# Hybrid decoder step on one core: the weight sum of the feed-forward block by an accumulating DMA, its three differences on VectorE, queues reordered

## The chip, the cores and the metric

The kernel is written for one core of a Trainium2 chip and runs on one core. The metric is the device time of one execution in microseconds, median of several runs; lower is better.

## The reference, cut to what matters

One inference step of a two-layer decoder, for 512 prompt tokens and 8 single-token samples with the same weights. Layer 0 mixes by attention and mLSTM heads, layer 1 by a recurrent block; after each mixer comes a SwiGLU feed-forward block, and after each of these four sub-layers a layer normalization. The change touches the first product of the feed-forward block alone:

```python
def ffn(u, li):
    gate, up = jnp.split(u @ w_ffn_in[li], 2, axis=-1)     # 1024 x 5632
    return (jax.nn.silu(gate) * up) @ w_ffn_out[li]        # 2816 x 1024

xp = post_norm(xp, ffn(up, li), mod_p[5], li, 1)
```

All of it is float32. The kernel keeps that precision by splitting each operand into a high part (rounded to fp32r) and a low part (the rest) and adding three matmuls: high x high, high x low, low x high.

## The kernel before

Activations lie transposed, features on the 128 partitions; the 520 columns (512 tokens, 8 samples) are two column halves of HT = 260. TensorE multiplies a 128x128 weight tile by 260 columns at a time.

**Stages.** The work goes in stages; each stage is a list of weight chunks. The feed-forward block of layer l has four: fi{l}0 (11 chunks), fo{l}0 (8), fi{l}1 (11), fo{l}1 (8). A chunk of fi holds the weights of 128 gate and 128 up features, for all 1024 input features: 1 MB in one of four raw buffers (NRAW), loaded by SyncE in two DMAs as [partition, k of 8, gate or up, 128]. Chunk c of the whole program uses raw buffer c mod 4, and its load waits (raw_free) until the chunk four before is through with its low parts.

**Seven products instead of eight.** In fi, all chunks but 0 and 1 of fi{l}0 (40 in all, `split_seven`) are computed by a Strassen-like scheme (the Winograd form). The chunk is a 2x2 block matrix: a11 (k 0 to 3, gate), a12 (k 4 to 7, gate), a21 (k 0 to 3, up), a22 (k 4 to 7, up), each 128x512 numbers in SBUF. The token matrix is likewise cut in 2x2, by feature halves and column halves. Seven block products, each of 4 k times 3 = 12 matmuls, replace eight. Their weight sides, in the order b = 0 to 6, are a11; S = a21 + a22; S - a11; a12 - (S - a11); a11 - a21; a12; a22.

**Who makes what.** For each block b, ScalarE makes the high part (`hi7(c, b)`, L1335) from its source in the raw buffer or in wsum, and VectorE the low part (`lo7(c, b)`, L2257). Before the change S is made on GpSimd into a buffer of its own, wsum (`weight_sum` part 0, L961), and a11 - a21 too, in the place of a21 (part 1, L963). VectorE makes the other two right behind `lo7(c, 0)` and `lo7(c, 1)`: S - a11 in the place of a11 (L2263), a12 minus that in the place of wsum (L2265). The buffer wsum lies in the memory of the second weight slot (whi[1]), so part 0 waits until its last user there is through: for the first chunk of fi{l}1 that is the last chunk of fo{l}0, for the first one of fi10 chunk 1. High and low parts have one buffer for each block, which holds the chunk being multiplied; `block_free` makes `hi7(n, b)` wait for product b of the chunk before.

**Evacuation.** Products accumulate in PSUM. Of a chunk c, ScalarE copies three intermediate sums out of the way (`copy_product` 0, 1, 2, L1522), after products 0, 1 and 2; TensorE starts blocks 2, 3 and 4 only after them. VectorE adds product sums in `add12` (L2562, after product 3) and `add22` (L2570, after product 4); block 6 waits for add22. Then ScalarE applies silu to both column halves (`silu_sums`, L1531 and L1534), VectorE multiplies by the up half (`gated_first` L2577, `gated_second` L2585), ScalarE makes the high part of the result (`high_h`, L1486) and VectorE its low part (`low_h`, L2538). For chunks 0 and 1 of fi{l}0 the corresponding steps are silu_of and gated_h.

**The order is written out by hand.** Every engine works through its queue in order. In the steady loop (step c, next chunk n = c + 1) ScalarE's queue is: copy 0, hi 6 of c, hi 0 of n, copy 1, hi 1 of n, copy 2, high_h of c - 1, hi 2 to 5 of n, keep (fi{l}0 only, L1415), both silus. VectorE's: gated_second of c - 1, lo 5 and 6 of c, lo 0 and 1 of n with a difference behind each, add12, low_h of c - 1, add22, lo 2 and 3 of n, gated_first, lo 4 of n.

GpSimd's queue, `ffn_sums(r)`, runs once per layer: small work on the samples, both parts for chunk 2, the four token sums (`token_sum`, 128x1040, L979 to L988), and then, for t = 0 to 7, both parts for chunk 3 + t and `keep_normalized(t)` (L1018, 128x520: part of what the residual needs later), and the parts for the eleven chunks of fi{l}1. Before and after that it works in the layer normalizations (L916 to L948).

**Starts.** Chunks 0 and 1 of fi{l}0 are multiplied while VectorE is still making the low tokens (`gained` L2479 and `low_tokens` L2486), tile by tile; TensorE follows them (`first_two_by_halves`, L3157). At the end of fo{l}0 the parts of the first chunk of fi{l}1 are made in the loop over its last two chunks: blocks 0 to 3 while chunk 7 is multiplied, 4 to 6 behind it.

## Time and profile before

| | us |
|---|---|
| median of 3 runs | 1551.78 |
| lowest, highest | 1549.71, 1552.03 |
| the profiled execution | 1551.36 |
| its span, first to last instruction | 1549.3 |

| engine | busy us | share of the span | instructions |
|---|---|---|---|
| TensorE (PE) | 1376.3 | 89% | 11764 |
| VectorE (DVE) | 1070.4 | 69% | 1599 |
| ScalarE (ACT) | 700.7 | 45% | 1180 |
| GpSimd (POOL) | 456.3 | 29% | 397 |

The chain that ended last is 34% VectorE, 28% TensorE, 5% ScalarE, 1% GpSimd. The mean granted TensorE clock is 0.95 of full. "L2257" is line 2257 of the kernel; "[0.36 <-ACT silb L1531]" behind an instruction means that its engine sat idle for 0.36 us before it, and what ended that. Matmuls overlap: one is shown as 0.28 us long and the next starts 0.12 us after it.

### The profile page before, as it was taken

Reading aid. Unit: us, or ns where it says so; the run is one execution under the profiler, and the core shown is the slowest. Engines: PE = TensorE matmul, PEld = TensorE weight load, DVE = VectorE, ACT = ScalarE, POOL = GpSimd, SP = SyncE. Lnnn points to the kernel's source line nnn. Section 1 sums busy time; section 2 is a strip of 40 time slices with the busy share of each in tenths; the row PEclk is TensorE's granted clock in tenths of the full one; section 3 lists DMA queues with packets and bytes.
Section 4 is the critical chain, followed back from the end, with each engine's and each line's share of the span. In section 5 each row is a group of like instructions: output and inputs, shape, how many; then the busy total and the mean of one; then the engine's idle time right before and its main releaser. Section 6 shows DMA issues by size and latency. Waiting matters only on the chain.

```text
span 1549.3 us, 30521 instructions
## 1 busy us (share of the span) xinstructions
PE 1376.3 (89%) x11764; PEld 1308.6 (84%) x11764; DVE 1070.4 (69%) x1599; ACT 700.7 (45%) x1180; POOL 456.3 (29%) x397
## 2 busy tenths in 40 slices
PE   4999978889997798989999989988968899899996
PEld 4899957666887698989999889988867889899995
DVE  4523268754757998449984888895769983499756
ACT  1211153234423666226653366892436661266524
POOL 2000031311174332012214536553553320133154
PEclk8999999899897899999999999998988999999998
DMA  9632296668330122323323212313402324233311
GB/s 319 213 95 55 84 334 236 234 244 303 112 109 1 55 81 75 105 80 109 100 76 111 82 41 90 108 36 98 136 1 55 100 71 115 82 85 97 94 38 56
DMA packets 213509, 175.04 MB, mean 113 GB/s; under 512 B 9079, under 2 KB 183932, under 8 KB 213252
## 3 DMA queue, kind: packets, MB, share of 16 engines
q1 hardware_dynamic: 208448, 160.13, 33.5%
q0 software_dynamic: 4800, 13.23, 2.5%
q8 instruction: 72, 1.18, 0.3%
q14 instruction: 49, 0.40, 0.1%
q10 hardware_dynamic: 140, 0.09, 0.0%
HBM read 167.87 MB, written 5.63 MB: 112 GB/s over the span
## 4 chain that ended last, share of the span: by engine, by line
DVE 34%; PE 28%; ACT 5%; issue 2%; POOL 1%; ACTq 0%; DVEq 0%; POOLq 0%
PE ps L3148 15%; DVE wlo L2257 12%; PE ps L3307 5%; PE ps L3157 4%; PE ps L3177 3%; DVE gn L2479 2%; ACT whi L1335 2%; DVE wsum L2265 2%; DVE raw L2263 2%; DVE hb L2577 2%; DVE wlo L2249 1%; DVE HL L2538 1%; DVE xc L2706 1%; DVE tL L2553 1%; DVE UL L2486 1%
## 5 line engine op out<-in xcount | busy, mean ns | idle before, releaser
L3307 PE MATMUL ps<-UH,whi 128*128 128x260 f32 x640 | 186.9, 292 | 28.6 <-DVE hb L2570 28.5
L1322 ACT ACTIVATE whi<-raw 128x1408 fp32r<-128x1408 f32 (+3 forms) x64 | 101.3, 1582 | 241.4 <-PE ps L3148 186.8
L2257 DVE TENSOR_TENSOR wlo<-raw,whi 128x512 fp32r<-128x512 f32 x200 | 187.1, 936 | 8.9 <-ACT whi L1335 2.2
L961 POOL TENSOR_TENSOR wsum<-raw 128x512 f32<-128x512 f32 x40 | 54.5, 1361 | 438.7 <-DVE wlo L2257 262.0
L3307 PE MATMUL ps<-UL,whi 128*128 128x260 f32 x640 | 183.4, 287 | 0.0
L3307 PE MATMUL ps<-UH,wlo 128*128 128x260 f32 x640 | 182.7, 285 | 0.0
L3307 PE MATMUL ps<-tH,whi 128*128 128x260 f32 x480 | 139.9, 292 | 34.8 <-DVE tL L2546 13.5
L1335 ACT ACTIVATE whi<-raw 128x512 fp32r<-128x512 f32 x200 | 126.4, 632 | 65.9 <-DVE raw L2263 37.3
L2249 DVE TENSOR_TENSOR wlo<-raw,whi 128x1408 fp32r<-128x1408 f32 (+3 forms) x64 | 130.6, 2040 | 36.4 <-ACT whi L1322 35.6
L3307 PEld LDWEIGHTS ps<-UH,whi 128*128 128x128 f32 x640 | 123.5, 193 | 35.5 <-issue 34.3
L3307 PE MATMUL ps<-tH,wlo 128*128 128x260 f32 x480 | 139.2, 290 | 0.0
L3307 PE MATMUL ps<-tL,whi 128*128 128x260 f32 x480 | 138.8, 289 | 0.0
L3148 PE MATMUL ps<-UH,whi 128*128 128x260 f32 x624 | 126.8, 285 | 6.9 <-DVE wlo L2249 6.9
L3148 PE MATMUL ps<-UH,wlo 128*128 128x260 f32 x624 | 126.1, 284 | 0.0
L3148 PE MATMUL ps<-UL,whi 128*128 128x260 f32 x624 | 126.0, 284 | 0.0
L3307 PEld LDWEIGHTS ps<-tH,whi 128*128 128x128 f32 x480 | 93.3, 194 | 37.2 <-issue 29.2
L3307 PEld LDWEIGHTS ps<-UL,whi 128*128 128x128 f32 x640 | 123.4, 193 | 0.0
L3307 PEld LDWEIGHTS ps<-UH,wlo 128*128 128x128 f32 x640 | 123.3, 193 | 0.0
L3148 PEld LDWEIGHTS ps<-UH,whi 128*128 128x128 f32 x624 | 96.8, 190 | 8.1 <-DVE wlo L2249 8.1
L3148 PE MATMUL ps<-HH,whi 128*128 128x260 f32 x484 | 97.4, 283 | 0.0
L3148 PE MATMUL ps<-HH,wlo 128*128 128x260 f32 x484 | 97.1, 282 | 0.0
L3148 PE MATMUL ps<-HL,whi 128*128 128x260 f32 x484 | 97.1, 282 | 0.0
(552 smaller groups left out, 3723.0 us busy)
## 6 DMA issues: line engine op xcount, KB each, us to landing
raw<-in_w_ada SPq DMA_DIRECT2D x96, 512.0 KB, 6.7
raw<-in_w_ffn_in SPq DMA_DIRECT2D x88, 512.0 KB, 5.1
raw<-in_w_in_even SPq DMA_DIRECT2D x24, 512.0 KB, 4.8
raw<-in_w_ffn_out SPq DMA_DIRECT2D x32, 384.0 KB, 4.1
raw<-in_w_ffn_out SPq DMA_DIRECT2D x32, 320.0 KB, 3.2
raw<-in_w_in_odd SPq DMA_DIRECT2D x20, 512.0 KB, 4.5
raw<-in_w_out_odd SPq DMA_DIRECT2D x16, 320.0 KB, 3.6
page<-in_cache_k POOLq DMA_DIRECT2D x16, 256.0 KB, 5.1
```

The lines of the kernel that those rows point to most:

```text
L961: ins = pool.tensor_tensor(wsum[:], a21, a22, ALU.add)
L1322: ins = nc.scalar.activation(whi[w][:, 0:f], raw[c % NRAW][:, 0:f], ACT.Identity)
L1335: nc.scalar.activation(seven_block(b)[0], seven_source(c, b), ACT.Identity).then_inc(seven_hi, 1)
L2249: ins = v.tensor_tensor(wl_[:, 0:f], raw[c % NRAW][:, 0:f], wh[:, 0:f].bitcast(F32), ALU.subtract)
L2257: v.tensor_tensor(low, seven_source(c, b), high.bitcast(F32), ALU.subtract).then_inc(seven_lo, 1)
L2263: ins = v.tensor_tensor(a11, wsum[:], a11, ALU.subtract)
L2265: ins = v.tensor_tensor(wsum[:], a12, a11, ALU.subtract)
L2479: v.scalar_tensor_tensor(gn_of(r, hf)[:, t, 0:HALF], xT[:, t, hf, 0:HALF], gain, rstd[:, hf, 0:HALF], ALU.mult, ALU.mult).then_inc(n_ready, 1)
L3148: ins = T.matmul(ps(g)[:, hf, 0:HT], wt(k, m), x[:, k, hf], start=(k == 0 and wt is wh and x is xh), stop=(k == s.k - 1 and wt is wl_))
L3157: ins = T.matmul(ps(g)[:, hf, 0:HT], wt(k, m), xt[:, k, hf], start=(k == 0 and wt is wh and xt is xh), stop=(k == s.k - 1 and wt is wl_), ...
L3177: ins = T.matmul(ps(g)[:, hf, 0:HT], w(k, m), x[:, k, hf], start=(i == 0 and w is wh and x is xh), stop=(i == s.k - 1 and w is wl_))
L3307: ins = T.matmul(out, wt[:, k], x, start=(b in (0, 1) and k == 0 and wt is wh and x is xh), stop=(k == 3 and wt is wl_), skip_group_check= ...
```

## The change

GpSimd no longer computes on the weights. It issues, for each of the 40 chunks, one DMA that reads a22 again from DRAM and adds it to a21 in the raw buffer, so that S stands in the place of a21; ScalarE waits for that DMA before hi 1. wsum is gone, and with it the wait for its memory. The sums of chunks 2 and 3 are issued ahead of the token sums, the others one chunk earlier than before relative to keep_normalized. VectorE makes all three differences in place: S - a11 over a21, a12 minus that over a11, a22 minus S - a11 (which is a11 - a21) over a21. ScalarE's and VectorE's queues are in another order: high_h and low_h come at the head of a step, keep before hi 2, the first silu between hi 3 and hi 4, the second between hi 4 and hi 5, lo 2 before add22. The whole diff:

```diff
--- before.py
+++ after.py
@@ -428,7 +428,6 @@
         tL = [at("tL0", [P, 4, HT], O_L, F32R), at("tL1", [P, 4, HT], O_L + 4 * HTB, F32R)]
         tL2 = [at("tL20", [P, 2, HT], O_L + 6 * HTB, F32R),
                nc.alloc_sbuf_tensor_at("tL21", [P, 2, HT], F32R, offset=CN0 + C_MASK * 4 + 2 * HTB)]
-        wsum = nc.alloc_sbuf_tensor_at("wsum", [P, 4, P], F32, offset=split_at + 4 * (SLOT + 1536))
         db = sml[:, 28:32]
 
         xr = at("xr", [P, KR, 2 * HT], 0)
@@ -456,7 +455,8 @@
 
         raw_loaded = [sem(f"raw_loaded{i}") for i in range(NRAW)]
         hi_done, lo_done = sem("hi_done"), sem("lo_done")
-        seven_hi, seven_lo, wsum_ready = sem("seven_hi"), sem("seven_lo"), sem("weight_sums_ready")
+        seven_hi, seven_lo = sem("seven_hi"), sem("seven_lo")
+        wsum_ready = [sem(f"weight_sum_ready{i}") for i in range(NRAW)]
         product_filled, copied, u3_used, pre_ready = sem("product_filled"), sem("product_copied"), sem("u3_used"), sem("pre_ready")
         wdiff_ready = sem("weight_differences_ready")
         silu_ready = sem("silu_of_sums")
@@ -543,7 +543,7 @@
 
             r = raw[c % NRAW][:].rearrange("p (k g m) -> p k g m", k=8, g=2)
             a11, a12, a21, a22 = r[:, 0:4, 0], r[:, 4:8, 0], r[:, 0:4, 1], r[:, 4:8, 1]
-            return (a11, wsum[:], a11, wsum[:], a21, a12, a22)[b]
+            return (a11, a21, a21, a11, a21, a12, a22)[b]
 
         def seven_block(b):
 
@@ -948,21 +948,13 @@
                     pool.tensor_tensor(x, x, mu[:, hf, 0:HALF], ALU.subtract).then_inc(d_ready, 1)
                     settled(pool, d_ready)
 
-            def weight_sum(n, part):
+            def weight_sum(n):
 
                 i = seven_index[n]
-                a11, a12, a21, a22 = (seven_source(n, b) for b in (0, 5, 4, 6))
-                if part == 0:
-                    pool.wait_ge(raw_loaded[n % NRAW], 32 * (n // NRAW + 1))
-                    if holder[n][1] not in seven_index:
-                        slot_free(pool, n, 1)
-                    if i >= 1:
-                        pool.wait_ge(seven_lo, 7 * i - 3)
-                    ins = pool.tensor_tensor(wsum[:], a21, a22, ALU.add)
-                else:
-                    ins = pool.tensor_tensor(a21, a11, a21, ALU.subtract)
-                ins.then_inc(wsum_ready, 1)
-                settled(pool, wsum_ready)
+                s = chunk_stage[n]
+                pool.wait_ge(raw_loaded[n % NRAW], 32 * (n // NRAW + 1))
+                pool.dma_start(seven_source(n, 1), weight_view(s)[s.chunks.index(n)][:, 4:8, 1],
+                               accum_op=ALU.add).then_inc(wsum_ready[n % NRAW], 16)
 
             def gn_samples(r, hf):
 
@@ -997,8 +989,8 @@
                 gn_samples(r, 0)
                 gn_samples(r, 1)
                 link(pool.tensor_tensor(db, B9[:, r + 1, 4:8, 0], B9[:, r + 1, 0:4, 0], ALU.subtract))
-                weight_sum(n0[2], 0)
-                weight_sum(n0[2], 1)
+                weight_sum(n0[2])
+                weight_sum(n0[3])
                 token_sum(r, 0)
                 token_sum(r, 1)
                 token_sum(r, 2)
@@ -1007,12 +999,11 @@
                 pool.wait_ge(rstd_ready, 2 * r + 2)
                 pool.wait_ge(ulo_ready, 8 + 16 * (r + 1))
                 for t in range(KD):
-                    for part in range(2):
-                        weight_sum(n0[3 + t], part)
+                    if t < KD - 1:
+                        weight_sum(n0[4 + t])
                     keep_normalized(t)
                 for n in n1:
-                    for part in range(2):
-                        weight_sum(n, part)
+                    weight_sum(n)
 
             def keep_normalized(t):
                 pool.tensor_tensor(xT[:, t], xT[:, t], rstd[:], ALU.mult).then_inc(kept_n, 1)
@@ -1328,10 +1319,10 @@
                 i = seven_index[c]
                 act.wait_ge(raw_loaded[c % NRAW], 32 * (c // NRAW + 1))
                 block_free(act, c, b)
-                if b in (1, 4):
-                    act.wait_ge(wsum_ready, 2 * i + (1 if b == 1 else 2))
-                if b in (2, 3):
-                    act.wait_ge(wdiff_ready, 2 * i + b - 1)
+                if b == 1:
+                    act.wait_ge(wsum_ready[c % NRAW], 16 * len([x for x in seven_index if x <= c and x % NRAW == c % NRAW]))
+                if 2 <= b <= 4:
+                    act.wait_ge(wdiff_ready, 3 * i + b - 1)
                 nc.scalar.activation(seven_block(b)[0], seven_source(c, b), ACT.Identity).then_inc(seven_hi, 1)
                 settled(act, seven_hi)
 
@@ -1522,14 +1513,18 @@
                 nc.scalar.activation(dst, ps(g)[:, src, 0:HT], ACT.Identity).then_inc(copied, 1)
                 settled(act, copied)
 
-            def silu_sums(s, c):
+            def silu_first(s, c):
 
                 i = seven_index[s.chunks[c]]
-                g = s.g0 + 2 * c
                 sil = ff_buffers(s, c)[0]
                 act.wait_ge(pre_ready, i + 1)
                 nc.scalar.activation(sil[:, 1], sil[:, 1], ACT.Silu).then_inc(silu_ready, 1)
                 settled(act, silu_ready)
+
+            def silu_second(s, c):
+
+                g = s.g0 + 2 * c
+                sil = ff_buffers(s, c)[0]
                 wait_filled(act, g)
                 free(nc.scalar.activation(sil[:, 0], ps(g)[:, 0, 0:HT], ACT.Silu), g)
                 act.wait_ge(freed[g % NGRP], g // NGRP + 1)
@@ -1566,30 +1561,35 @@
                         for b in range(5):
                             hi7(ch[3], b)
                         hi7(ch[3], 5)
-                        silu_sums(s, 2)
+                        silu_first(s, 2)
+                        silu_second(s, 2)
                         first = 3
                     for c in range(first, s.n):
                         k = k0 + c
                         n = ch[c + 1] if c + 1 < s.n else None
-                        copy_product(s, c, k, 0)
                         if c > 0:
                             hi7(ch[c], 6)
+                            high_h(s, c - 1, k - 1)
+                        copy_product(s, c, k, 0)
                         if n is not None:
                             hi7(n, 0)
                         copy_product(s, c, k, 1)
                         if n is not None:
                             hi7(n, 1)
                         copy_product(s, c, k, 2)
-                        if c > 0:
-                            high_h(s, c - 1, k - 1)
+                        if hf == 0:
+                            keep(2 * l, c - 3)
                         if n is not None:
-                            for b in range(2, 6):
-                                hi7(n, b)
+                            hi7(n, 2)
+                            hi7(n, 3)
                         else:
                             hi(f0)
-                        if hf == 0:
-                            keep(2 * l, c - 3)
-                        silu_sums(s, c)
+                        silu_first(s, c)
+                        if n is not None:
+                            hi7(n, 4)
+                        silu_second(s, c)
+                        if n is not None:
+                            hi7(n, 5)
                     high_h(s, s.n - 1, k0 + s.n - 1)
                     hi(f0 + 1)
                     s = st[f"fo{l}{hf}"]
@@ -2256,15 +2256,17 @@
                 dve.wait_ge(seven_hi, 7 * seven_index[c] + b + 1)
                 v.tensor_tensor(low, seven_source(c, b), high.bitcast(F32), ALU.subtract).then_inc(seven_lo, 1)
                 settled(dve, seven_lo)
-                if b < 2:
-                    a11, a12 = seven_source(c, 0), seven_source(c, 5)
-                    dve.wait_ge(wsum_ready, 2 * seven_index[c] + 2)
-                    if b == 0:
-                        ins = v.tensor_tensor(a11, wsum[:], a11, ALU.subtract)
-                    else:
-                        ins = v.tensor_tensor(wsum[:], a12, a11, ALU.subtract)
-                    ins.then_inc(wdiff_ready, 1)
-                    settled(dve, wdiff_ready)
+            def difference(c, j):
+
+                a11, a12, a21, a22 = (seven_source(c, b) for b in (0, 5, 4, 6))
+                if j == 0:
+                    ins = v.tensor_tensor(a21, a21, a11, ALU.subtract)
+                elif j == 1:
+                    ins = v.tensor_tensor(a11, a12, a21, ALU.subtract)
+                else:
+                    ins = v.tensor_tensor(a21, a22, a21, ALU.subtract)
+                ins.then_inc(wdiff_ready, 1)
+                settled(dve, wdiff_ready)
 
             g = use["tb"]
             wait_filled(dve, g)
@@ -2599,11 +2601,14 @@
                         if l == 1:
                             lo7(ch[2], 0)
                         lo7(ch[2], 1)
+                        difference(ch[2], 0)
+                        difference(ch[2], 1)
                         token_low(l, 0)
                         low_h(s, 0, k0)
                         gated_h(s, 1, k0 + 1)
                         token_low(l, 1)
                         lo7(ch[2], 2)
+                        difference(ch[2], 2)
                         low_h(s, 1, k0 + 1)
                         lo7(ch[2], 3)
                         token_low(l, 2)
@@ -2615,7 +2620,10 @@
                         add22(s, 2)
                         lo7(ch[3], 0)
                         lo7(ch[3], 1)
+                        difference(ch[3], 0)
+                        difference(ch[3], 1)
                         lo7(ch[3], 2)
+                        difference(ch[3], 2)
                         lo7(ch[3], 3)
                         gated_first(s, 2)
                         lo7(ch[3], 4)
@@ -2627,19 +2635,21 @@
                             gated_second(s, c - 1)
                             lo7(ch[c], 5)
                             lo7(ch[c], 6)
+                            low_h(s, c - 1, k - 1)
                         if n is not None:
                             lo7(n, 0)
                             lo7(n, 1)
+                            difference(n, 0)
+                            difference(n, 1)
                         add12(s, c)
-                        if c > 0:
-                            low_h(s, c - 1, k - 1)
+                        if n is not None:
+                            lo7(n, 2)
                         add22(s, c)
                         if n is not None:
-                            lo7(n, 2)
+                            difference(n, 2)
+                            lo7(n, 3)
                         else:
                             lo(f0)
-                        if n is not None:
-                            lo7(n, 3)
                         gated_first(s, c)
                         if n is not None:
                             lo7(n, 4)
@@ -2656,6 +2666,11 @@
                         else:
                             for b in range(4 * (c - s.n + 2), 7 if c == s.n - 1 else 4):
                                 lo7(s.c0 + s.n, b)
+                                if b == 1:
+                                    difference(s.c0 + s.n, 0)
+                                    difference(s.c0 + s.n, 1)
+                                if b == 2:
+                                    difference(s.c0 + s.n, 2)
                 ln_round(2 * l + 1)
 
             def per_tile(col, n=NS):

```

## Rows read from the trace of the kernel before

**Rows 1.** Chain that ended last: start us, length us, engine, tile, line, instructions.

```profile
538.80 11.87 PE ps L3307 x84
...
622.03 7.89 PE ps L3177 x66
...
629.93 55.27 PE ps L3148 x462
...
808.43 7.89 PE ps L3177 x66
```

**Rows 2.** Waits: who waited for whom; us in total, times, longest.

```profile
PE ps L3307 <- DVE hb L2570: 28.5, 32, 2.3
```

**Rows 3.** VectorE in time, fi01: start, length, line, out<-in, [idle before].

```profile
734.84 1.67 DVE L2257 TENSOR_TENSOR wlo<-raw,whi 128x512 fp32r<-128x512 f32 x1
...
737.00 2.65 DVE L2257 TENSOR_TENSOR wlo<-raw,whi 128x512 fp32r<-128x512 f32 x3
...
739.69 0.69 DVE L2263 TENSOR_TENSOR raw<-wsum,raw 128x512 f32<-128x512 f32 x1
...
745.44 1.66 DVE L2257 TENSOR_TENSOR wlo<-raw,whi 128x512 fp32r<-128x512 f32 x1
```

**Rows 4.** GpSimd in time, the same stretch.

```profile
734.51 1.44 POOL L961 TENSOR_TENSOR wsum<-raw 128x512 f32<-128x512 f32 x1 [7.47 <-DVE wlo L2257]
...
736.03 1.62 POOL L963 TENSOR_TENSOR raw<-raw 128x512 f32<-128x512 f32 x1
```

**Rows 5.** VectorE in time, fi00.

```profile
529.34 0.64 DVE L2577 TENSOR_TENSOR hb<-hb,silb 128x260 f32<-128x260 f32 x1 [1.09 <-ACT silb L1531]
...
588.11 1.38 DVE L2577 TENSOR_TENSOR hb<-hb,silb 128x260 f32<-128x260 f32 x1 [0.37 <-ACT silb L1531]
```

**Rows 6.** GpSimd in time, fi00.

```profile
578.79 1.65 POOL L1018 TENSOR_TENSOR xT<-xT,rstd 128x520 f32<-128x520 f32 x1
```

**Rows 7.** TensorE in time, starts of fi00 and fi10.

```profile
505.79 0.28 PE L3307 MATMUL ps<-UH,whi 128*128 128x260 f32 x1
...
530.19 0.39 PE L3307 MATMUL ps<-tH,whi 128*128 128x260 f32 x1 [1.74 <-ACT ps L1522]
...
1147.40 0.28 PE L3307 MATMUL ps<-UH,whi 128*128 128x260 f32 x1
...
1162.51 0.56 PE L3307 MATMUL ps<-tH,whi 128*128 128x260 f32 x1 [13.50 <-DVE tL L2546]
...
1183.69 0.38 PE L3307 MATMUL ps<-tH,whi 128*128 128x260 f32 x1 [1.00 <-ACT ps L1522]
```

**Rows 8.** GpSimd in time, starts of fi01 and fi10.

```profile
685.41 1.29 POOL L961 TENSOR_TENSOR wsum<-raw 128x512 f32<-128x512 f32 x1 [81.12 <-PE ps L3148]
...
1147.80 1.29 POOL L961 TENSOR_TENSOR wsum<-raw 128x512 f32<-128x512 f32 x1 [14.30 <-PE ps L3157]
```

**Rows 9.** TensorE in time, start of fi01.

```profile
689.62 0.41 PE L3307 MATMUL ps<-tH,whi 128*128 128x260 f32 x1 [3.01 <-DVE wlo L2257]
```

**Rows 10.** Windows: us, busy (x) of PE, PEld, DVE, ACT, POOL; PEclk; DMA.

```profile
689.00:693.00 4.00, 2.79 (x12) 2.49 (x12) 3.71 (x7) 3.08 (x5) 0.99 (x1) 0.61 0.00 0
```

**Rows 11.** DMA issues: out<-in, queue, count, KB each, median us to landing.

```profile
raw<-in_w_ffn_in SPq DMA_DIRECT2D x88, 512.0 KB, 5.1
...
page<-in_cache_k POOLq DMA_DIRECT2D x16, 256.0 KB, 5.1
...
Cs<-in_state_C POOLq DMA_DIRECT2D x1, 1024.0 KB, 12.8
```

**Rows 12.** Groups by form, ScalarE: count, busy us, mean ns.

```profile
L1486 ACT ACTIVATE HH<-hb 128x520 fp32r<-128x520 f32 x44 | 28.2, 641 | 12.9 <-DVE hb L2585 6.3 <-DVE hb L2532 5.3
```

**Rows 13.** VectorE in time, layer normalization before fi00.

```profile
491.39 2.49 DVE L2479 SCALAR_TENSOR_TENSOR gn<-xT,G,rstd 128x256 f32<-128x256 f32 x1
```

**Rows 14.** GpSimd in time, a DMA issue in the middle stage.

```profile
203.03 0.54 POOL L836 DMA_DIRECT2D out_k_prompt<-ktok  x1 [2.23 <-ACT vtok L1088]
```

**Rows 15.** VectorE in time, beside that issue.

```profile
203.21 0.68 DVE L1820 TENSOR_TENSOR rowc<-rows,rowc 4x512 f32<-4x512 f32 x1
```

## The prediction

> **What bounds the kernel now.** I read the chain of work that ended last first, for the order of the stages and their lengths, then the waits of TensorE, then each engine's instructions in order of time in single chunks. Each layer has a feed-forward block in two halves, fi{l}0 and fi{l}1, of 11 chunks each. Chunks 0 and 1 of fi{l}0 are computed directly; the other nine and all eleven of fi{l}1 go through seven block products, 84 matmuls a chunk, 40 chunks in all. Dense matmuls go at 55.27 us / 462 = 0.1196 us [rows 1], so 84 take 10.05 us: TensorE's floor for a chunk, a block of 12 being 1.44 us.
>
> In fi{l}1 a chunk takes 745.44 - 734.84 = 10.60 us [rows 3], and in that stretch VectorE's instructions follow each other with no idle time: VectorE sets the pace and TensorE waits a little each time for the addition of L2570 before its block 6, in both halves together 28.5 us in 32 waits [rows 2]. VectorE doesn't really have that much to do. A low part of 128x512 takes 0.69 us where GpSimd is still, as the difference at 739.69 [rows 3], but 1.66 to 1.67 us beside GpSimd's first addition, and the first of the three at 737.00, beside its second, takes 2.65 - 2 x 0.72 = 1.21 us [rows 3, 4] (0.72 is 0.69 with the step to the next). These two cost 0.98 + 0.52 = 1.50 us a chunk. Without them VectorE would need 9.10 us.
>
> In fi{l}0 the eight last chunks take longer: from block 6 of chunk 3 (538.80) to the end (622.03) it is 83.2 us for seven chunks' worth of work, 11.9 a chunk [rows 1]. GpSimd does a third instruction per chunk, keep_normalized [rows 6], and VectorE both loses time to it and sits idle for silu_first on ScalarE [rows 5], which is queued behind four high parts and keep.
>
> Two more places. At the start of fi{l}1 the sum block cannot be written before TensorE is through with the last chunk of fo{l}0, since wsum lies in the second slot: GpSimd waits 81 us for it and adds at 685.41 [rows 8]; TensorE stands 3.01 us [rows 9] and comes back at the lower level of its clock, 0.61 granted [rows 10], matmuls every 0.21 us. At the start of fi10 the same wait ends at 1147.80 [rows 8], all four token sums are queued behind it, and TensorE stands 13.50 us [rows 7].
>
> **The change part by part.**
>
> 1. *Two GpSimd additions per chunk go; the third difference comes to VectorE.* In fi{l}1 VectorE's chunk becomes 10.60 - 1.50 + 0.72 = 9.82 us, under TensorE's 10.05. What is late next is TensorE itself, if the new order holds. I walked one chunk with block 0 at 0 and products done at 1.6, 3.1, 4.5, 5.9, 7.4, 8.8 and 10.2: gated_second at 0.2, lo 5, lo 6 and low_h to 2.8, lo 0 to 3.6, lo 1 pinned by its high part (product 1) at 4.2 to 4.9, two differences to 6.3, add12 to 6.8, lo 2 to 7.5, add22 to 8.0, against block 6 at 8.6. Then difference 2, lo 3, gated_first and lo 4 to 10.6, 0.4 behind, which the pinned lo 1 takes up again. No wait on TensorE is left, with 0.6 us to spare. ScalarE has 8 us of work at most and no long idle wait in it. So fi{l}1 goes from 808.43 - (629.93 + 55.27) = 123.2 us [rows 1] to 11 x 10.05 + 0.6 for uneven spots = 111.1 us. That includes the stall at its start: the sum now needs no slot, blocks 0 to 3 are made during the last chunk of fo{l}0, and by the same walk block 4's low part is there 3 us before its turn. Gain 12.1 us, twice: 24.2.
>
> 2. *fi{l}0, chunks 3 to 10.* keep_normalized stays on GpSimd and now runs some 9 us after chunk start, when the load behind it has landed (5.1 us, [rows 11]), beside VectorE's low parts and differences. Its price lies between 0.52 and 0.98 us, as for the two instructions of [rows 3, 4]; the upper is the nearer since a two-SBUF-input instruction is then under way nearly always. I take 0.95. silu_first comes before two of the high parts, so the wait of [rows 5] goes. From block 6 of chunk 3 to that of chunk 9 there are six chunks of 9.82 and five keeps: 58.9 + 4.8 = 63.7 us, still VectorE's, then block 6 and the last chunk on TensorE, 11.1. Together 74.8 against 83.2: gain 8.4, twice: 16.8. The copy of ScalarE's keep hides as before.
>
> 3. *The new order at the entry to that loop.* For chunk 3, copy_product 0 used to be the next thing after silu_second; TensorE waited 1.74 us for it (block 2 at 530.19, [rows 7]). Now high_h(2) stands ahead of it, and that waits for gated_first (529.34, 0.64 long, [rows 5]), lo 4 (0.69) and gated_second (at most 0.64) on VectorE and takes 0.64 itself [rows 12]: 2.3 to 2.6 us later, and 0.7 more for difference 2 on VectorE's queue, and up to 0.98 if a keep falls there. TensorE would stand 1.7 + 2.7 to 1.7 + 4.2 us, say 4.8. After 3.01 us at the handover the clock came back low [rows 9, 10], after 1.74 here it had not; so I expect the low level for about as long as there, some 30 matmuls at 0.21 instead of 0.12, 2.8 us. As part of the delay is taken up before block 6 (before it TensorE waited 2 us there as well), I put 3.7 us at block 6 of chunk 3, bounds 0 and 6. Loss 3.7, twice: 7.4.
>
> 4. *Start of fi{l}0.* Layer 0: the two additions go from the time in which VectorE makes the low tokens that TensorE follows one by one: about 2 x 0.9 = 1.8 us gained; two differences now on VectorE's busy stretch cost 1.4, the two additions gone later give back 1.1: net +1.5. Layer 1: the walk from block 0 of chunk 2 to block 2 of chunk 3 took 1183.69 - 1147.40 = 36.3 us and in layer 0, where the slot was free, 530.19 - 505.79 = 24.4 [rows 7]. The difference, 11.9, goes; but token sum 0 is now no longer held back and falls onto the low tokens, as in layer 0, where one 0.48 us instruction took 2.49 [rows 13]: -2.0, and -0.3 for the differences. Net +9.6. Layers together +11.1.
>
> 5. *The accumulating DMA.* Nothing in the trace adds in a DMA. Landing: the nearest in size is a page of 256 KB, 5.1 us; the far end is 1 MB in 4096 short rows, 12.8 us [rows 11]. I take 7. It has time: the raw buffer of chunk n is freed at lo 6 of chunk n - 4, its load lands about 6 us later, and hi 1 of chunk n comes three chunks and 1.4 us after that freeing: 3 x 10.05 + 1.4 - 6.5 = 25 us for the sum. At the start of fi10 GpSimd is free to issue it at 1147.80 - 14.30 = 1133.5 [rows 8], and ScalarE wants it some 3 us before block 0 of chunk 2 begins at 1147.40 [rows 7], 10.6 us later; TensorE's need is another 5 us away. Cost nothing, as long as it lands in those times. Issue: GpSimd spends 0.54 us on one [rows 14]. Whether that takes VectorE's time as an addition does: the 0.68 us instruction with two SBUF inputs at 203.21 ran beside such an issue at its usual length [rows 14, 15]. It is on 4 partitions only, but I take 0; the upper bound is 0.98 per issue.
>
> Sum: 24.2 + 16.8 - 7.4 + 11.1 = 44.7 us. The profiled execution took 1551.36 us (span 1549.3), the median of the runs is 1551.78, 0.4 more. 1551.8 - 44.7 = 1507.1 us.
>
> **The rivals.**
>
> A. *The issue on GpSimd takes VectorE's time like an addition.* For it: every GpSimd computation does [rows 3, 4]; against it: [rows 14, 15], weak evidence. At 0.75 a chunk VectorE is at 10.57 in fi{l}1, hardly better than 10.60, which costs 0.52 x 11 x 2 = 11.4 us, and 0.75 x 6 x 2 = 9 in fi{l}0: 1527.5 us (1535 at 0.98).
>
> B. *No low clock and little delay at chunk 3* (part 3 costs nothing): 1499.7 us.
>
> C. *Slower: the DMA sum lands late.* Per chunk T = (6.5 + L - 1.4) / 3 once L passes 25 us; the gain of 44.7 is eaten over 36 chunks at 1.25 us more a chunk, that is L of about 29 us; at L = 33, T is 12.7, and 36 x 2.65 = 95 us come on top, with some 20 each at the starts: 1640 us. For it: the adding must read both sides and no row has its price; against: twice the worst landing of [rows 11] is 25.6. The Trainium skill's page "DMA: Bandwidth & Descriptors" (Anatomy of one DMA) would give 2.6 us for a plain transfer of this size issued on GpSimd; the row has 5.1.
>
> D. *VectorE still sets the pace by the order of its queue* (the walk has only 0.23 us per chunk and 0.6 at block 6): 10.3 instead of 10.05 in fi{l}1 costs 5.5: 1513 us.
>
> E. *keep_normalized costs VectorE its whole length*, 1.65 us [rows 6] where I take 0.95. Against it: a 1.44 us addition cost 0.98, the next 0.52 [rows 3, 4]. It would cost 0.7 x 5 x 2 = 7 us: 1514. The Trainium skill's page "SBUF — State Buffer" (Who interferes with whom) has this rule: of a VectorE instruction with two inputs in SBUF and a GpSimd instruction that reads SBUF, the one that starts second waits for the first to end. In the rows above the loss always stays under the length of the GpSimd instruction.
>
> F. *Nothing gained*, for a cause that I don't see, within 0.2%: about 1552.
>
> **How the numbers follow.** Forecast with part 3 as told, 0.48; D 0.08; E 0.04; B 0.10; A 0.18; C 0.08; F 0.04. The likeliest is 1507. The range takes in B and most of A: 1498 to 1528, leaving out C, F and a little at each end, 0.2. A measurement of this kernel tells 0.2% from no change. Faster: 0.48 + 0.08 + 0.04 + 0.10 + 0.18 = 0.88; same 0.04; slower 0.08.
>
> **What would show it.** In fi{l}1: chunks of 10.05 us, no wait of TensorE for L2570, all low parts at 0.69, handover without the stall. Chunks of 10.5 with low parts over 0.9 beside a GpSimd issue: A. ScalarE waiting for the DMA before the high part of block 1 in every chunk: C. In fi{l}0: low parts slow once a chunk, chunks of 10.8 falling to 10.05 at the end; TensorE standing over 4 us before block 2 of chunk 3 and then 0.5 to 0.6 granted. At 1147: the 13.50 us gone to about 4. The forecast is wrong above all if the landing of the DMA is far over 13 us, or if the clock falls elsewhere.

## The result, and the profile after

The changed kernel takes 1525.28 us (median of 4 runs, 1523.42 to 1531.36) against 1550.94 before in the same comparison: a ratio of 0.984, 95% interval 0.981 to 0.987. That is 1.6% less, clear of the scatter, and inside the range given, but 18 us over the forecast of 1507: of the 44.7 us expected, 25.7 came. The profiled execution took 1526.53 us, its span is 1524.9 (before 1549.3), so the two spans differ by 24.4 us.

The second halves did what was forecast. From the chain of work that ended last, of the changed kernel (start us, length us, what), to be read against [rows 1]:

```profile
637.07 55.25 PE ps L3163 x462
692.33 110.79 PE ps L3322 x924
803.11 7.89 PE ps L3192 x66
...
1326.82 110.81 PE ps L3322 x924
```

All eleven chunks of fi01 are one unbroken run of 924 matmuls, 110.79 us, a chunk every 10.07. The handover from fo00 is without a wait. Nothing of VectorE's or ScalarE's is in it. GpSimd and VectorE in one of these chunks (start us, length us, engine, line, operation, tiles, count, idle time before; L956 is the accumulating DMA's issue):

```profile
740.93 1.29 POOL L956 DMA_DIRECT2D raw<-in_w_ffn_in  x1 [8.74 <-DMA raw<-in_w_ffn_in]
751.05 1.28 POOL L956 DMA_DIRECT2D raw<-in_w_ffn_in  x1 [8.82 <-DMA raw<-in_w_ffn_in]
...
750.67 0.69 DVE L2267 TENSOR_TENSOR raw<-raw 128x512 f32<-128x512 f32 x1
751.40 0.69 DVE L2257 TENSOR_TENSOR wlo<-raw,whi 128x512 fp32r<-128x512 f32 x1
752.12 0.43 DVE L2579 TENSOR_TENSOR hb<-hb,silb 128x260 f32<-128x260 f32 x1
```

The low part at 751.40 lies wholly inside the issue of 1.28 us and takes its usual 0.69. An issue by itself takes nothing from VectorE. It does take GpSimd 1.28 us, where the plain one of [rows 14] took 0.54. The landing, from the table of DMA issues (KB each, us to landing):

```profile
raw<-in_w_ffn_in SPq DMA_DIRECT2D x88, 512.0 KB, 5.1
raw<-in_w_ffn_in POOLq DMA_DIRECT2D x40, 256.0 KB, 4.6
```

4.6 us, 7.5 at most over the 40; the forecast took 7 and had 25 to spend. No engine waits for it.

The first halves did not do it. What TensorE waited for (engine, line, released by: us in total, times, longest):

```profile
PE ps L3322 <- ACT ps L1513: 22.9, 10, 5.5
PE ps L3322 <- DVE wlo L2257: 18.8, 2, 9.6
```

The wait for add22 [rows 2], 28.5 us before, has all but gone. In its place stand L1513, copy_product 0, before block 2 of chunk 3 and of later chunks of the first halves, and L2257 before block 2 of chunk 2, once per layer. Single waits and the clock behind the first two, in windows (stretch, length, busy us of each engine with the instructions, granted clock):

```profile
521.27 0.56 PE L3322 MATMUL ps<-tH,whi 128*128 128x260 f32 x1 [9.19 <-DVE wlo L2257]
539.86 0.58 PE L3322 MATMUL ps<-tH,whi 128*128 128x260 f32 x1 [5.39 <-ACT ps L1513]
565.11 0.38 PE L3322 MATMUL ps<-tH,whi 128*128 128x260 f32 x1 [1.63 <-ACT ps L1513]
590.00 0.58 PE L3322 MATMUL ps<-tH,whi 128*128 128x260 f32 x1 [2.41 <-ACT ps L1513]
...
1156.40 0.56 PE L3322 MATMUL ps<-tH,whi 128*128 128x260 f32 x1 [9.62 <-DVE wlo L2257]
```

```profile
521.00:525.00 4.00, 3.73 (x17) 3.76 (x18) 3.76 (x8) 1.31 (x3) 0.00 (x0) 0.50 0.31 39
...
539.00:543.00 4.00, 3.14 (x14) 3.15 (x15) 3.79 (x6) 2.44 (x6) 0.00 (x0) 0.50 0.41 121
```

And the cause, one chunk of fi00 on GpSimd and VectorE (L1009 is keep_normalized, L2579 gated_first):

```profile
559.72 1.30 POOL L956 DMA_DIRECT2D raw<-in_w_ffn_in  x1 [10.81 <-DMA raw<-in_w_ffn_in]
560.54 1.83 POOL L1009 TENSOR_TENSOR xT<-xT,rstd 128x520 f32<-128x520 f32 x1
...
559.45 0.69 DVE L2257 TENSOR_TENSOR wlo<-raw,whi 128x512 fp32r<-128x512 f32 x1
560.17 2.49 DVE L2579 TENSOR_TENSOR hb<-hb,silb 128x260 f32<-128x260 f32 x1
562.70 0.69 DVE L2257 TENSOR_TENSOR wlo<-raw,whi 128x512 fp32r<-128x512 f32 x1
```

keep is shown from 560.54, before the issue ends at 561.02, and gated_first, which takes 0.43 us elsewhere, takes 2.49. It lost 2.06 us, more than the 1.83 that keep is shown as long, and twice the 0.98 of an addition in [rows 3, 4]. gated_second, high_h and copy_product 0 follow from it in that order: hence the waits for L1513.

Fourteen of the sixteen keeps stand behind an issue like this one, and cost the VectorE instruction beside them 1.18 to 2.28 us, 1.85 on average. The last keep of each layer has no issue ahead of it and stands behind another keep; there the low part beside it takes 1.67 us, a loss of 0.98:

```profile
584.45 3.28 POOL L1009 TENSOR_TENSOR xT<-xT,rstd 128x520 f32<-128x520 f32 x2
...
586.61 1.67 DVE L2257 TENSOR_TENSOR wlo<-raw,whi 128x512 fp32r<-128x512 f32 x1
```

Where the 24.4 us of the two profiled executions lie, against the steps of the prediction (us, minus is faster; stretches between the same events in both traces):

| stretch | forecast | measured |
|---|---|---|
| up to gn of the second half, layer 0 (code unchanged) | 0 | +4.1 |
| gn to block 0 of chunk 2, layer 0 / layer 1 | -1.8 / +2.0 | -0.8 / +3.8 |
| block 0 of chunk 2 to block 6 of chunk 3 | +4.0 / -7.9 | +6.3 / -5.3 |
| block 6 of chunk 3 to the end of fi{l}0 | -8.4 / -8.4 | -2.3 / -3.0 |
| fi{l}1 | -12.1 / -12.1 | -12.5 / -12.5 |
| the rest | 0 | -2.2 |

The first row is no effect of the change, whose first instruction comes later. Here are the windows of 200 to 300 us, the kernel before first, then after:

```profile
200.00:300.00 100.00, 79.18 (x950) 62.49 (x951) 76.50 (x157) 36.80 (x92) 18.59 (x29) 0.90 0.77 264
```

```profile
200.00:300.00 100.00, 79.57 (x871) 63.12 (x871) 76.42 (x154) 35.77 (x89) 17.18 (x28) 0.85 0.77 266
```

950 matmuls at 0.90 granted against 871 at 0.85. One of the experiments below, keep_landed, had 0.85 there too and came to fi00 nearly as late. Over all fourteen traces the point at which the first row ends lies between 482.5 and 489.3 us. Where a few us matter, stages are compared below and not spans; the length of fi00 or fi10 is then from block 0 of chunk 2 to the end of the stage (116.1 us for fi00 before the change, 120.02 after).

### The profile page after: what moved, and what is told of

Its sections match the earlier page's. It is cut to its first block, busy times and chain, and to the rows that moved or that the text cites. A ratio compares the mean times of both kernels' runs of the same rounds, so it can differ in the third digit from the quotient of the medians.

```text
span 1524.9 us, 30410 instructions
## 1 busy us (share of the span) xinstructions
PE 1365.9 (90%) x11764; PEld 1303.8 (86%) x11764; DVE 1057.9 (69%) x1639; ACT 701.8 (46%) x1180; POOL 390.3 (26%) x357
## 3 DMA queue, kind: packets, MB, share of 16 engines
q8 instruction: 72, 1.18, 0.3%
## 4 chain that ended last, share of the span: by engine, by line
PE 44%; DVE 21%; ACT 4%; issue 1%; POOL 0%; ACTq 0%; DVEq 0%; POOLq 0%
PE ps L3322 21%; PE ps L3163 15%; PE ps L3172 4%; DVE wlo L2257 3%; PE ps L3192 3%; DVE gn L2481 2%; DVE UL L2488 1%; DVE wlo L2249 1%; DVE xc L2721 1%; DVE hb L2579 1%; DVE tL L2555 1%; DVE rstd L2454 1%; DVE xc L2756 1%; DVE raw L2267 1%; DVE xc L2755 1%
## 5 line engine op out<-in xcount | busy, mean ns | idle before, releaser
L1326 ACT ACTIVATE whi<-raw 128x512 fp32r<-128x512 f32 x280 | 177.6, 634 | 119.1 <-DVE raw L2267 58.1
L2257 DVE TENSOR_TENSOR wlo<-raw,whi 128x512 fp32r<-128x512 f32 x280 | 203.8, 728 | 15.8 <-ACT whi L1326 5.5
L3322 PE MATMUL ps<-UH,whi 128*128 128x260 f32 x640 | 182.7, 286 | 1.0 <-DVE hb L2572 1.0
L956 POOL DMA_DIRECT2D raw<-in_w_ffn_in x40 | 51.8, 1321 | 427.7 <-DMA raw<-in_w_ffn_in 425.4
L3163 PE MATMUL ps<-UH,whi 128*128 128x260 f32 x624 | 126.1, 283 | 6.9 <-DVE wlo L2249 6.9
L3322 PEld LDWEIGHTS ps<-tH,whi 128*128 128x128 f32 x480 | 93.5, 195 | 44.9 <-DVE wlo L2257 24.9
```

The costliest lines, as they stand in the source:

```text
L956: pool.dma_start(seven_source(n, 1), weight_view(s)[s.chunks.index(n)][:, 4:8, 1], accum_op=ALU.add).then_inc(wsum_ready[n % NRAW], 16)
L1326: nc.scalar.activation(seven_block(b)[0], seven_source(c, b), ACT.Identity).then_inc(seven_hi, 1)
L2257: v.tensor_tensor(low, seven_source(c, b), high.bitcast(F32), ALU.subtract).then_inc(seven_lo, 1)
L3163: ins = T.matmul(ps(g)[:, hf, 0:HT], wt(k, m), x[:, k, hf], start=(k == 0 and wt is wh and x is xh), stop=(k == s.k - 1 and wt is wl_))
L3322: ins = T.matmul(out, wt[:, k], x, start=(b in (0, 1) and k == 0 and wt is wh and x is xh), stop=(k == 3 and wt is wl_), skip_group_check= ...
```

## The experiments

Two theories stood against each other above all. Theory I in the expectations: keep_normalized, queued right behind an issue, is what costs VectorE 2 us and more. Theory III: the new order of the queues does it, high_h and low_h at the head of a step, with the wait that this makes at chunk 3. Each edit is against the changed kernel unless said otherwise; "before" was measured beside each group at 1551.75, 1552.74, 1550.45 and 1553.16 us, so medians of different groups that lie under 3 us apart are not told apart.

**keep_gap.** GpSimd holds each keep back until low part 6 of chunk 3 + t is made:

```diff
                         weight_sum(n0[4 + t])
+                    pool.wait_ge(seven_lo, 7 * seven_index[n0[3 + t]] + 7)
                     keep_normalized(t)
```

> The changed kernel with one wait more on GpSimd: keep_normalized(t) waits until low part 6 of chunk 3 + t is done, so it no longer runs directly behind the issue of an accumulating DMA, but 4 us or more after it. Theory I (in the changed kernel a keep costs VectorE 1.9 to 2.3 us because it is queued right behind the issue and takes the port before the issue is over): VectorE's loss per keep falls to between 0.5 and 1.0 us, TensorE's waits before block 2 in fi00 and fi10 (1.3 to 2.4 us a chunk) fall under 0.7, and the time falls by 8 to 12 us, to about 1515. Theory II (a keep costs whichever VectorE instruction comes behind it the rest of its own length, issue or no issue): a loss of 1.3 to 1.7 us per keep, and 1 to 4 us gained, 1522 to 1524.

1502.91 us (1500.06 to 1507.86), ratio 0.969 (0.965 to 0.973): one wait more, 22 us less, about twice the 8 to 12 expected, and 4 us under the forecast for the change. fi00 takes 109.51 us instead of 120.02, chunk 4 10.34, chunks 5 to 9 10.84 each. The same two engines in one chunk:

```profile
552.67 1.80 POOL L1010 TENSOR_TENSOR xT<-xT,rstd 128x520 f32<-128x520 f32 x1 [7.42 <-DVE wlo L2258]
554.77 1.30 POOL L956 DMA_DIRECT2D raw<-in_w_ffn_in  x1 [0.30 <-POOL xT L1010]
...
552.62 0.70 DVE L2541 TENSOR_TENSOR HL<-hb,HH 128x520 fp32r<-128x520 f32 x1
553.35 2.40 DVE L2258 TENSOR_TENSOR wlo<-raw,whi 128x512 fp32r<-128x512 f32 x2
```

Two low parts in 2.40 instead of 1.42 us: 0.98 lost, where the forecast had 0.95 and theory II 1.3 to 1.7. The issue right behind keep does no harm; it is keep right behind the issue that does.

**no_keep.** keep's multiplication is reduced to its first column, so that part of the computation is left out:

```diff
-                    keep_normalized(t)
+                    x = xT[:, t, :, 0:1]
+                    pool.tensor_tensor(x, x, rstd[:, :, 0:1], ALU.mult).then_inc(kept_n, 1)
```

> The changed kernel without the work of keep_normalized in fi00 and fi10: of each tile GpSimd multiplies only the first column of each half, so layer 0's and layer 1's residual is not normalized. What all contention by keep costs. From block 6 of chunk 3 to the end of fi00 80.8 us should become 6 x 10.05 + 11.6 = 72, in both layers 17 to 18 us, and 2 to 4 more where keeps 0 and 1 fall on chunk 2: 1503 to 1508. If the chunks of fi00 stay over 10.5 us, it is not keep that slows them but the new order.

1497.13 us (1496.79 to 1499.68), ratio 0.965, 6 us under the least expected. fi00 105.40, every chunk from chunk 4 on at 10.07. So the eight keeps of each layer cost the changed kernel 28 us together, and keep_gap 6.

**h_back.** high_h and low_h at their old places in the step, the rest as changed:

```diff
-                            high_h(s, c - 1, k - 1)
                         copy_product(s, c, k, 0)
 ...
                         copy_product(s, c, k, 2)
+                        if c > 0:
+                            high_h(s, c - 1, k - 1)
```

(and low_h behind add12 in the same way.)

> The changed kernel with high_h and low_h at their old places in the steady loop (behind copy 2 on ScalarE, behind add12 on VectorE), everything else as changed. Theory III (TensorE's stall before block 2 of chunk 3, 5.4 us, and those of 1.3 to 2.4 us in the chunks after it come from high_h, which stands ahead of copy 0 and waits for gated_second): the 5.4 us fall to 2 to 3 and the clock stays up, the smaller waits before block 2 vanish, 6 to 12 us gained: 1513 to 1519. Rival (VectorE sets the pace of fi00 and fi10 in any order): the waits only move to before block 6, and the time stays within 3 us of 1525. In fi01 and fi11, where nothing is late, no difference: 10.05 us a chunk.

1533.67 us (1529.13 to 1534.3): slower than the changed kernel, which neither side expected. The new place is worth 0.41 us in every chunk of the second halves: fi01's chunks take 10.48 instead of 10.07, and TensorE waits before block 6 for add22 again, a little at a time:

```profile
736.73 0.39 PE L3324 MATMUL ps<-UH,whi 128*128 128x260 f32 x1 [0.18 <-DVE hb L2573]
747.21 0.38 PE L3324 MATMUL ps<-UH,whi 128*128 128x260 f32 x1 [0.17 <-DVE hb L2573]
```

The wait before block 2 of chunk 3 is 3.27 us here and 5.39 in the changed kernel, but what was a wait there comes back at block 6 in each later chunk. In sum the old order makes fi00 2.1 us and fi10 0.9 us shorter than in the changed kernel: that much of the missing 19 us theory III can have, and no more. As the main cause of the lost time it has fallen.

**sum_on_gpsimd.** The sum by GpSimd in place, everything else as changed:

```diff
-                pool.dma_start(seven_source(n, 1), weight_view(s)[s.chunks.index(n)][:, 4:8, 1],
-                               accum_op=ALU.add).then_inc(wsum_ready[n % NRAW], 16)
+                a21, a22 = seven_source(n, 1), seven_source(n, 6)
+                pool.tensor_tensor(a21, a21, a22, ALU.add).then_inc(wsum_ready[n % NRAW], 16)
```

> The changed kernel with the sum made by GpSimd in place (128x512 in the raw buffer) instead of by the DMA: what the DMA alone is worth, beside the freed slot, the differences and the order. A chunk of fi01 becomes 9.82 us plus what the addition costs VectorE: 10.8 us at the 0.98 us that an addition cost before, 11.1 at its full length of 1.3. So fi01 and fi11 get longer by 8 to 12 us each, fi00 and fi10 by 0 to 5: 1543 to 1555. If the time stays near 1525, the DMA is worth nothing and the gain came from the slot and the order.

1537.47 us (1535.54 to 1538.92), 5.5 us better than the least expected. fi01 takes 116.49 us, a chunk 10.87:

```profile
742.51 1.29 POOL L957 TENSOR_TENSOR raw<-raw 128x512 f32<-128x512 f32 x1 [9.69 <-DMA raw<-in_w_ffn_in]
...
742.57 1.79 DVE L2258 TENSOR_TENSOR wlo<-raw,whi 128x512 fp32r<-128x512 f32 x1
```

The low part loses 1.10 us, and 9.82 + 1.10 = 10.92. The DMA is worth 5.7 us in each second half, and in the first halves nothing (119.08 with the addition, 120.02 with the DMA). The rows of fi00 say why: keep stands right behind the addition here and costs 0.99, gated_first taking 1.42 instead of 0.43:

```profile
558.75 1.64 POOL L1010 TENSOR_TENSOR xT<-xT,rstd 128x520 f32<-128x520 f32 x1
...
559.25 1.42 DVE L2580 TENSOR_TENSOR hb<-hb,silb 128x260 f32<-128x260 f32 x1
```

The addition ahead of it costs 0.98, together 1.97, and an issue with keep behind it in the same place cost 2.06. So behind a computation keep has its usual price, in an otherwise unchanged kernel, and what the DMA saves keep takes back.

**keep_landed.** This tells the issue from the place: keep waits until the DMA issued just before it has landed, and so falls neither right behind the issue nor beside low part 6:

```diff
                         weight_sum(n0[4 + t])
+                        pool.wait_ge(wsum_ready[n % NRAW], ...)   # the sum just issued
                     keep_normalized(t)
```

> The changed kernel, with one wait added on GpSimd: keep_normalized(t) waits until the accumulating DMA issued right before it has landed (4.6 us on average), so it no longer starts while that issue is under way, but also not beside low part 6 as in keep_gap. Theory I (what costs VectorE 2 to 3 us instead of 1 is that keep starts right behind the issue, wherever it falls): VectorE loses about 1.0 us per keep, chunks 4 to 9 of the first halves take 10.8 to 10.9 us, the stage fi00 109 to 111 us as in keep_gap (109.51), total about 1503 (1499 to 1508). Rival (keep_gap gained because keep falls beside low parts instead of beside gated_first and gated_second, from which high_h and copy 0 follow): the place of 4 to 6 us later decides, the stage stays at 115 us or more, total 1515 or more.

1508.4 us (1505.14 to 1515.03). fi00 111.85 and fi10 112.48 us. The profiled execution was the longest of the four and entered fi00 4.3 us later than keep_gap's, so the stages say it better: they are 8.2 and 7.3 us shorter than in the changed kernel.

```profile
543.87 1.30 POOL L956 DMA_DIRECT2D raw<-in_w_ffn_in  x1 [6.84 <-DMA raw<-in_w_ffn_in]
548.70 1.31 POOL L1011 TENSOR_TENSOR xT<-xT,rstd 128x520 f32<-128x520 f32 x1 [3.53 <-DMA raw<-in_w_ffn_in]
...
548.88 1.70 DVE L2542 TENSOR_TENSOR HL<-hb,HH 128x520 fp32r<-128x520 f32 x1
```

keep is 1.31 us long, low_h beside it loses 1.00. The distance from the issue decides, not what VectorE does at the time. The place has a small part too: the stages are 2.3 and 2.4 us longer than in keep_gap. All of that comes ahead of block 6 of chunk 3 (36.2 us from block 0 of chunk 2 in fi00, 33.4 in keep_gap), where three keeps fall here and one in keep_gap.

**keep_dve.** keep on VectorE, behind low part 4, on a semaphore of its own; GpSimd only issues:

```diff
                             lo7(n, 4)
+                            if hf == 0:
+                                keep_v(c - 2)
```

> The changed kernel with keep_normalized on VectorE, behind low part 4 of the next chunk, on a semaphore of its own; GpSimd only issues DMAs in these stages. Theory I: a two-input instruction of 128x520 costs VectorE 0.70 us where GpSimd is still, against 0.98 for the delay that the GpSimd keep costs in keep_gap. The chunk of chunks 4 to 9 becomes 9.82 + 0.70 = 10.5 us against 10.84 there, the stage fi00 about 107.5, total about 1499 (1496 to 1503). Rival (the delay by GpSimd's keep falls partly into VectorE's idle time, an own instruction does not): 10.8 us or more a chunk and 1503 or more.

1504.52 us (1502.59 to 1507.1): as keep_gap within the scatter, 5.5 above the 1499 expected. The loop came as worked out, nearly (10.63 a chunk for 10.5), so the rival's reason failed too; but chunk 3 takes 17.0 and 18.3 us in the two layers instead of 16.5: TensorE's wait before block 2 of chunk 3 is 5.39 us there, 4.64 in keep_gap.

**gap_copy_first.** keep_gap, and in chunk 3 alone copy_product 0 ahead of high_h:

```diff
+                            if hf == 0 and c == first:
+                                copy_product(s, c, k, 0)
                             high_h(s, c - 1, k - 1)
-                        copy_product(s, c, k, 0)
+                        if hf == 1 or c > first:
+                            copy_product(s, c, k, 0)
```

> keep_gap, and on ScalarE, in chunk 3 of the first halves alone, copy_product 0 stands ahead of high_h of chunk 2 again. Theory III, in the form that h_back leaves (the new place costs nothing inside the loop but one stall at its entry): the wait of 4.64 us before block 2 of chunk 3 falls to 1.5 to 2.5 us and TensorE stays at its full clock behind it, the first stage of each layer is 2.5 to 5 us shorter than in keep_gap (109.51 and 110.06), total 1494 to 1498. Rival (VectorE sets the pace of the loop from its first chunk on, so that the stall is only the place where TensorE waits for it): the wait goes elsewhere, the stages stay within 1 us, total 1501 to 1505.

1501.68 us (1500.28 to 1502.78), fi00 109.40 for 109.51, fi10 110.04 for 110.06: nothing, as the rival had it. The waits, the one of keep_gap first, then those here:

```profile
530.55 0.38 PE L3323 MATMUL ps<-tH,whi 128*128 128x260 f32 x1 [4.64 <-ACT ps L1514]
```

```profile
528.41 0.38 PE L3326 MATMUL ps<-tH,whi 128*128 128x260 f32 x1 [3.29 <-ACT ps L1514]
536.37 0.38 PE L3326 MATMUL ps<-UH,whi 128*128 128x260 f32 x1 [1.34 <-DVE hb L2576]
```

and the windows behind each, in the same order:

```profile
530.00:534.00 4.00, 3.45 (x17) 3.46 (x18) 3.83 (x6) 2.70 (x7) 2.76 (x2) 0.62 0.48 137
```

```profile
528.00:532.00 4.00, 3.24 (x25) 3.05 (x26) 3.83 (x6) 3.00 (x7) 1.81 (x1) 1.00 0.16 39
```

4.64 became 3.29 + 1.34, in sum the same. The clock granted behind it rose from 0.62 to 1.00, and that brought nothing either, since VectorE sets the pace from there on.

**gap_token_first.** keep_gap, and token sum 0 ahead of the two issues at the start instead of right behind them:

```diff
+                token_sum(r, 0)
                 weight_sum(n0[2])
                 weight_sum(n0[3])
-                token_sum(r, 0)
```

> keep_gap, and at the start of each first half GpSimd's token sum 0 stands ahead of the two DMA issues instead of right behind them. Theory I: token sum 0 then starts right behind no issue and costs VectorE about 2.0 us as in the kernel before, where the instruction beside it took 2.49 instead of 0.48 us, and not 3.5 (UL took 4.0). From the centering of the second half to block 0 of chunk 2, 1 to 2 us less per layer; total about 1500 (1498 to 1502). Rival (token sum 0 costs VectorE the same wherever it starts, or starts earlier and hits an instruction that TensorE follows more closely): no change or longer, 1502 to 1505.

1501.25 us (1498.97 to 1502.31). The same mechanism at another place. In keep_gap, with the sum behind the issues, UL takes 4.01 us; here the instruction it meets takes 2.49, as in [rows 13]:

```profile
488.54 4.01 DVE L2489 SCALAR_TENSOR_TENSOR UL<-gn,B,UH 128x256 fp32r<-128x256 f32 x1
```

```profile
489.36 2.63 POOL L971 TENSOR_TENSOR ts<-gn,gn 128x1040 f32<-128x1040 f32 x1 [2.05 <-DVE gn L2482]
...
489.77 2.49 DVE L2482 SCALAR_TENSOR_TENSOR gn<-xT,G,rstd 128x256 f32<-128x256 f32 x1
```

1.5 us saved on VectorE, in layer 0 1.1 of it at block 0 of chunk 2 (18.73 us from gn instead of 19.83), and 0.5 given back in fi00: too little for the medians to tell.

**keep_late.** All eight keeps of GpSimd behind the last low part of fi{l}0, ScalarE's keeps in the groups of fo{l}0, where VectorE stands 4.8 us of 7.9. The DMAs of the sums are issued one after another ahead of them, and VectorE waits for ScalarE's keep tile by tile in fo{l}0:

```diff
+                pool.wait_ge(seven_lo, 7 * seven_index[n0[-1]] + 7)
+                for t in range(KD):
+                    keep_normalized(t)
 ...
                     for c in range(s.n):
+                        if hf == 0:
+                            keep(2 * l, c)
```

> The changed kernel with the eight keep_normalized and ScalarE's keeps out of the loop: GpSimd does all eight after low part 6 of the last chunk, ScalarE one at each of the eight groups of fo00 and fo10, where VectorE stands 4.8 us of 7.9 in each. Theory I (in the loop a keep costs VectorE 1 us even at its best, and the loop is VectorE's): chunks 4 to 10 go at TensorE's 10.07 us as in no_keep, whose first stages took 105.40 and 106.00 us; 105 to 107 here, since the eight fall beside the last chunk, where VectorE has little to do; fo00 stays at 63.2 us; total 1495 to 1499, some 5 us under keep_gap and 28 under the changed kernel. Rival (the eight in a row of 10.4 us take VectorE's time just before fo00 needs its first low parts and residual, TensorE stands there 3 us or more each time): 1500 to 1505.

1496.88 us (1488.82 to 1499.08), ratio 0.965. fi00 105.77, fi10 105.94, as without keeps. The eight run in one row and the low parts beside them are longer, but no wait of TensorE comes of it:

```profile
602.61 13.23 POOL L1010 TENSOR_TENSOR xT<-xT,rstd 128x520 f32<-128x520 f32 x8 [33.27 <-DVE wlo L2258]
...
607.88 2.20 DVE L2250 TENSOR_TENSOR wlo<-raw,whi 128x1408 fp32r<-128x1408 f32 x1
610.12 1.41 DVE L2582 TENSOR_TENSOR hb<-hb,silb 128x260 f32<-128x260 f32 x1
```

**keep_late_token_first.** Both edits together.

> keep_late with token sum 0 ahead of the two issues, as in gap_token_first, where it took 1.1 us from the way to block 0 of chunk 2 and gave back 0.5 in the stage behind. If the gain comes where the loop is TensorE's, both should be 0.6 to 1.1 us shorter per layer than in keep_late: total 1493 to 1498. Rival (what is gained ahead of the stage is given back in VectorE's stretch of chunks 2 and 3 in full): as keep_late within 0.5 us.

1493.31 us (1492.25 to 1495.67), ratio 0.963 (0.961 to 0.965). From gn to block 0 of chunk 2 it is 2.1 and 1.0 us less than in keep_late, while fi00 and fi10 take 105.37 and 106.35 us for 105.77 and 105.94. The medians are 3.6 us apart, but keep_late's four runs spread over 10.

**before_no_keep.** The kernel before, with keep reduced as in no_keep, that part of the computation left out.

> The kernel before with keep_normalized reduced to its first column (that part of the computation is left out). It prices keep where it ran behind a GpSimd addition and not behind a DMA issue: in the changed kernel leaving it out took 14.6 us from fi00 (120.02 to 105.40). Theory I (adding behind an addition costs about 1 us more per keep, the long delays belong to the issue): chunks of 10.6 to 10.9 us, fi00 106 to 110 us instead of 116.1, total 1537 to 1541. Rival (keep costs as much in the kernel before as in the changed one, 2 us a chunk, and the change only kept that): fi00 102 us or less is not possible with chunks of 10.6 us set by VectorE, so the sign of it would be that the waits at chunk 3 and at block 6 vanish with the keeps and the total falls to 1530 or lower.

1542.03 us (1538.83 to 1547.09, 6 runs): a little over the 1537 to 1541 expected. The keeps cost the kernel before 8.4 us by the medians (interval 4.2 to 10.7) and 9.3 by the lengths of fi00 and fi10. The chunks are 11.38 us and not the 10.6 to 10.9 expected, so of the 1.32 us by which fi00's chunks were longer than fi01's (11.92 and 10.60) keep had 0.54:

```profile
558.51 1.30 POOL L961 TENSOR_TENSOR wsum<-raw 128x512 f32<-128x512 f32 x1 [8.04 <-DVE wlo L2259]
559.88 1.36 POOL L963 TENSOR_TENSOR raw<-raw 128x512 f32<-128x512 f32 x1
...
558.71 1.38 DVE L2579 TENSOR_TENSOR hb<-hb,silb 128x260 f32<-128x260 f32 x1 [0.37 <-ACT silb L1533]
560.12 1.67 DVE L2259 TENSOR_TENSOR wlo<-raw,whi 128x512 fp32r<-128x512 f32 x1
```

Both additions cost nearly a full microsecond here (0.95 and 0.98), and VectorE waits 0.37 for silu_first: 9.10 + 0.95 + 0.98 + 0.37 = 11.40.

**late_copy_first.** keep_late_token_first with copy_product 0 first in chunk 3.

> keep_late_token_first with copy_product 0 ahead of high_h in chunk 3 of the first halves, as in gap_copy_first. There the wait of 4.64 us split into 3.29 at block 2 and 1.34 at block 6, TensorE kept its full clock, and the stage was no shorter, since VectorE set the pace behind it. Here the loop behind is TensorE's at 10.07 us a chunk. Theory I (the two waits are both VectorE's lateness and stay 4.6 us in sum; only the low clock behind the one long wait, 18 or so matmuls at 0.21 instead of 0.12 us, is given back): fi00 and fi10 1 to 2 us shorter than 105.37 and 106.35, total 1490 to 1493. Rival (block 6 waits longer by what the faster matmuls won, VectorE being late in any case): the stages within 0.3 us, total as keep_late_token_first, 1493 to 1494.

1492.32 us (1489.11 to 1495.72), ratio 0.961 (0.958 to 0.964). fi00 104.21 and fi10 104.75 us, 1.2 and 1.6 shorter, as theory I had it in size but not in its reason: the wait is 3.28 instead of 4.64 and no wait at block 6 of chunk 3 takes its place, while the clock behind it came back low all the same:

```profile
525.00:529.00 4.00, 3.77 (x20) 3.56 (x21) 3.81 (x6) 2.78 (x6) 0.00 (x0) 0.66 0.47 91
```

The gain is that of the shorter wait, 1.36 us. In a loop that is TensorE's, the edit counts; the medians are too close to show it by themselves. This version and keep_late_token_first beat both kernels, the changed one by 33 and 32 us.

## Why the prediction was right or wrong

**Part 1, second halves: right.** 110.8 us for 111.1, no wait, 10.07 us a chunk. h_back shows that the order of the queues is needed for it (10.48 without), which the walk assumed and did not price.

**Part 5, the DMA: right where it mattered.** Landing 4.6 us for 7, no effect of the issue on an instruction beside it (751.40 above), so rival A (0.18) did not happen, nor C. The issue takes GpSimd 1.28 us instead of 0.54, and this term was called free. By itself it was. That 1525 us lies inside the range is luck: the range reached to 1528 for the sake of A.

**Part 2, first halves: the step that failed.** It said that keep "now runs some 9 us after chunk start", beside low parts, at 0.52 to 0.98 us. The bounds came from additions that follow a computation or an idle stretch [rows 3, 4], and the part did not ask what keep now stands behind. In the change it stands right behind an issue, and there the price is 1.85 us on average (1.18 to 2.28), outside both bounds. The same eight instructions per layer, priced by leaving them out (us for both layers; in all but the first row against no_keep):

| where keep runs | cost |
|---|---|
| before: behind a GpSimd addition | 1550.4 - 1542.0 = 8.4 |
| after: right behind the issue | 1525.3 - 1497.1 = 28.2 |
| when that DMA has landed | 1508.4 - 1497.1 = 11.3 |
| on VectorE | 1504.5 - 1497.1 = 7.4 |
| beside low part 6 | 1502.9 - 1497.1 = 5.8 |
| behind the last chunk | 1496.9 - 1497.1 = -0.3 |

The prediction's own sum gives the keeps 74.8 - (6 x 10.05 + 11.1) = 3.4 us a layer, 6.8 in both, where 28.2 were measured (the losses of the sixteen VectorE instructions beside them add up to 27.9): 21.4 too little, and 19 are missing. So the other terms together came out some 2 us better than told, and not each as told (parts 3 and 4 below; the 11.1 us for block 6 and the last chunk should be 1.44 + 10.05 = 11.5 by the prediction's own figures, and no_keep has 11.7). Without keeps in either kernel the change is worth 1542.0 - 1497.1 = 44.9 us; that this is the 44.7 forecast with keeps is chance. With keep away from the issue the chunk of part 2 is 10.84, forecast 9.82 + 0.95 = 10.77: the sum was right but for that one price.

**Part 3, the entry to the loop: the mechanism was there, the price wrong.** A wait before block 2 of chunk 3 of 5.39 us (forecast 4.8) and the low clock behind it, 0.50 granted, as told. But a wait of TensorE in a stretch that VectorE paces is not a loss on top: in gap_copy_first it was moved and the clock kept, and nothing changed. In no_keep, where the wait is 4.64 us and the clock behind it low too, the stretch from block 0 of chunk 2 to block 6 of chunk 3 takes 33.5 us in layer 0, 0.5 more than in the kernel before, for the +4.0 forecast. Only with the keeps out of the loop is a shorter wait worth something, 1.2 and 1.6 us, under half of the 3.7 taken. That the stretch was 6.3 us longer in the changed kernel is keep again, 5.8 of it (39.3 us against 33.5): keeps fell beside low parts of chunks 2 and 3, for which part 3 had 0.98 at most. The low part at 518.43 takes 2.73 us, and TensorE stood 9.19 us for it (521.27), 4.40 in the kernel before and 5.18 without keeps.

**Part 4, the starts: too good by 1.0 us in layer 0 and 1.8 in layer 1 up to block 0.** Behind block 0 in layer 1 the stretch is 2.6 us worse than told with the keeps, and 3.0 better without them (no_keep, -10.9). The stall of 13.50 us before block 1 [rows 7] went, as told, but TensorE stands 9.62 us before block 2 (1156.40) where about 4 were forecast; without keeps it is 5.81. And token sum 0 was taken at 2.0 us of VectorE's time from [rows 13] although the change puts it right behind two issues: 4.02 instead of 0.48. That is the same oversight as in part 2.

**Rival E had the cause, at 0.04.** It said that keep might cost VectorE its whole length, and spoke against itself with rows of additions. Where keep is queued behind an issue, VectorE loses about all of the length that keep is shown with: 2.06 us at 560.17, where that is 1.83, and 1.85 on average for keeps of 1.8. The Trainium skill's page "SBUF — State Buffer" (Who interferes with whom) says that of two such instructions the later one waits for the other to end; the row at 560.17 agrees as far as the loss goes, but gated_first is shown as starting first and still was the one to wait, which the page does not lead one to expect. The size given to E (7 us) was too small because it was counted for five keeps of a layer, and all eight fell on VectorE's time.

The rows tell one thing more. As the profile shows the times, the VectorE instruction beside each of the sixteen keeps stands from its own start until keep ends, less 0.13 to 0.20 us: at 560.17 it loses 560.54 + 1.83 - 560.17 - 0.14 = 2.06 us, in keep_gap 552.67 + 1.80 - 553.35 - 0.14 = 0.98, and the same sum gives the 0.98 and 0.52 of [rows 3, 4] to 0.01. What differs is who is held. In keep_gap the instruction at 552.62 is under way when keep starts and runs its usual 0.70 us, and only the next one is held. Behind an issue the one under way is held as well, if both its inputs are in SBUF and it starts 0.22 us or more after the issue. From the start of the issue to the end of keep it is 2.61 to 2.66 us in all fourteen cases, 1.30 for the issue and 1.31 for a keep by itself. So keep ends as if it began when the issue is over, and VectorE stands for part of the issue too, though an issue without a computation behind it costs it nothing. What holds VectorE in that time no run here tells.

## What to carry to other kernels

A GpSimd computation queued right behind a DMA that GpSimd issues cost VectorE up to twice what it costs alone; put a wait between them, or the computation ahead of the issue, before asking for anything larger. When an edit changes what stands ahead of an instruction on its queue, price that instruction anew, though the edit does not touch it. And ask of each wait whether the stretch behind it belongs to the waiting engine: only then is removing it worth its length.

## What the runs showed of the hardware that was not expected

- keep_normalized (128x520, two inputs in SBUF) costs a VectorE instruction 0.98 to 1.02 us when it starts by itself (keep_gap) or behind another computation (559.25 in sum_on_gpsimd, 586.61 in the changed kernel), and 1.18 to 2.28 right behind an issue; a token sum of 128x1040 2.0 by itself, 3.5 behind two issues. The issue alone costs VectorE nothing.
- An issue of 256 KB with accumulation takes GpSimd 1.28 to 1.30 us, where a plain one took 0.54 [rows 14], and lands after 4.6 us. Whether the adding or the shape of the transfer makes the difference was not tried.
- Behind a wait of 5.39 us TensorE was granted 0.50, behind 4.64 us 0.62. Behind 3.29 us it had the full clock in gap_copy_first, behind 3.28 us 0.66 in late_copy_first, and [rows 9, 10] have 0.61 behind 3.01, so the length of the wait alone does not decide it; what else does was not tried.
